# One decoder layer with attention, convolution and experts: the part between attention and the first expert is ordered anew

## The reference

```python
mod = silu(c) @ w_ada + b_ada                 # shift, scale, gain for both halves (6 x 1024)
sh1, sc1, g1, sh2, sc2, g2 = split(mod, 6)
mix = mixer(x * (1 + sc1) + sh1)              # attention A (4 heads), attention B (8 heads), conv C, then w_out
x = layer_norm(ALPHA * x + g1 * mix, ln_g[0], ln_b[0])
h = x * (1 + sc2) + sh2
logits = h @ w_router + b_router              # 32 experts, best 4, softmax over the 4
y = sum over the 4 of gate * expert(h)        # expert: 1024 -> 2048, clamped SwiGLU, 1024 -> 1024
x = layer_norm(ALPHA * x + g2 * y, ln_g[1], ln_b[1])
```

## Time and profile before

| | us |
|---|---|
| three runs | 1288.34, 1290.24, 1290.70; median 1290.24 |
| profiled execution | 1290.84 |
| its span | 1289.1 |
| PE busy | 1026.4 |
| DVE busy | 317.9 |
| ACT busy | 183.3 |
| DMA queue of SP | 449.26 MB, 86.0% of 16 engines' span |

### The profile page before, as it was taken

The page is one execution under the profiler, slowest core; times in us unless marked ns, Lnnn a source line. Parts: engine busy times, 40 slices in busy tenths (PEclk is TensorE's granted clock), DMA queues, the critical chain, the costliest instruction groups (busy, mean ns, idle before and its releaser), DMA issues.

```text
span 1289.1 us, 30824 instructions
## 1 busy us (share of the span) xinstructions
PE 1026.4 (80%) x12341; PEld 487.2 (38%) x12342; DVE 317.9 (25%) x1042; ACT 183.3 (14%) x512; POOL 55.0 (4%) x137
## 2 busy tenths in 40 slices
PE   3799897498997877868698969997896897867872
PEld 2455653343443332423343433442343343332331
DVE  0295456712211211211121211121111111111215
ACT  0101332411111100101011101110111111110101
POOL 2900000000004000000000000000000000000000
PEclk9799899599998977988899989999898999888987
DMA  9987773279999999999799899089979979999993
GB/s 325 335 293 267 222 274 157 102 294 421 420 420 420 420 420 421 420 420 396 329 421 419 338 419 418 8 339 420 413 319 419 421 326 420 421 419 421 422 420 138
DMA packets 78075, 455.05 MB, mean 353 GB/s; under 512 B 9067, under 2 KB 16661, under 8 KB 28769
## 3 DMA queue, kind: packets, MB, share of 16 engines
q1 hardware_dynamic: 73840, 449.26, 86.0%
q10 hardware_dynamic: 4145, 4.41, 1.1%
HBM read 451.59 MB, written 2.61 MB: 352 GB/s over the span
## 4 chain that ended last, share of the span: by engine, by line
PE 38%; DMA 24%; SPq 22%; DVE 8%; issue 5%; ACT 2%; ACTq 0%; DVEq 0%
DMA w<-in_w_e_out 22%; PE bank L1677 15%; SPq L407 10%; PE bank L1705 8%; SPq L410 6%; PE bank L1658 3%; SPq L388 2%; PE comb L1637 2%; PE bank L1548 1%; DMA w<-in_ln_b 1%; SPq L374 1%; DMA w<-in_w_ada 1%; PE bank L1693 1%; PE bank L1670 1%; SPq L483 1%
## 5 line engine op out<-in xcount | busy, mean ns | idle before, releaser
L1677 PE MATMUL bank<-w,mt 128*32 128x512 f32 x3264 | 389.6, 622 | 45.8 <-DMA w<-in_w_e_in 45.8
L1705 PE MATMUL bank<-w,mt 128*32 128x256 f32 x3264 | 197.2, 387 | 45.8 <-DMA w<-in_w_e_out 31.8
L1677 PEld LDWEIGHTS bank<-w,mt 128*32 128x32 f32 x3264 | 96.4, 113 | 301.2 <-issue 215.8
L1224 DVE TENSOR_SCALAR mt<-bank 128x256 f32<-128x256 f32 x51 | 21.6, 424 | 718.6 <-PE bank L1677 718.6
L1705 PEld LDWEIGHTS bank<-w,mt 128*32 128x32 f32 x3264 | 98.7, 111 | 127.6 <-DMA w<-in_w_e_out 48.1
L1658 PE MATMUL bank<-pick,hb 128*128 128x32 bf16 x2448 | 80.2, 179 | 67.3 <-issue 64.2
L1658 PEld LDWEIGHTS bank<-pick,hb 128*128 128x128 bf16 x2448 | 75.4, 97 | 91.8 <-issue 91.8
L823 ACT ACTIVATE mt<-mt 128x256 f32<-128x256 f32 x51 | 21.3, 417 | 493.5 <-DVE mt L1224 493.5
L1637 PE MATMUL comb<-mt,gpickT 32*128 32x256 f32 x832 | 80.9, 462 | 0.5 <-ACT mt L830 0.5
L1659 PE MATMUL bank<-pick,hb 96*128 96x32 bf16 x408 | 72.5, 179 | 0.0
L1637 PEld LDWEIGHTS comb<-mt,gpickT 32*128 32x128 f32 x832 | 35.4, 199 | 49.2 <-issue 46.5
(11 more groups left out here) (335 smaller groups left out, 816.2 us busy)
## 6 DMA issues: line engine op xcount, KB each, us to landing
w<-in_w_e_in SPq DMA_DIRECT2D x256, 1024.0 KB, 26.0
w<-in_w_e_out SPq DMA_DIRECT2D x128, 1024.0 KB, 21.3
w<-in_w_ada SPq DMA_DIRECT2D x12, 2048.0 KB, 11.0
w<-in_w_in SPq DMA_DIRECT2D x3, 2048.0 KB, 21.9
w<-in_w_in SPq DMA_DIRECT2D x2, 1024.0 KB, 21.5
w<-in_w_out SPq DMA_DIRECT2D x4, 512.0 KB, 10.1
w<-in_w_out SPq DMA_DIRECT2D x2, 1024.0 KB, 12.3
w<-mod_rows SPq DMA_DIRECT2D x4, 512.0 KB, 6.6
```

Of the source, the lines that this page charges most:

```text
L1677: ins = mm(quarter(bank[0][SLOTS * q:SLOTS * (q + 1), :], 0), xT[:, SLOTS * k:SLOTS * (k + 1)], quarter(slot[s], q), start=False, stop=(k ...
L1705: ins = mm(bank[0][SLOTS * q:SLOTS * (q + 1), 0:256], hid, slot[s][:, D * (k % 2) + 256 * q:D * (k % 2) + 256 * (q + 1)], start=False, sto ...
```

## The change

It does the following, in one kernel:

- the sample's values go on three column tiles of PE (24 products of 128 columns), with three ACT copies; the first projection waits for its input piece by piece, and the sample's input lies in quarters on 128 partitions;
- attention takes all of tile 0 first, then tile 1; the output projection starts after step 6 and has 28 products within attention instead of 20; the sample's projection comes ahead of the last four products of tile 1;
- DVE waits for `ld["brow"]` ahead of the first `maxima`; the first tile's layer norm sits in steps 11, 12 and 13 of attention;
- the sample's layer norm works on 128 partitions by 256 columns; the layer norm's scaling is folded into two passes for each half; the tiles are taken in the order 0, 2, 1; `choose` has 9 small operations;
- the first block is written out ahead of the loops; the visiting order is multiplied behind its first products, and `cum`, `order` and the clearing of sums come inside it; expert 0 has at least two blocks (`minblk`);
- the end: two loads on a semaphore `gain`, four on `final`; the last layer norm is done by DVE in two fused passes, with ACT doing the root only; POOL applies the mean and root to the rows kept for it.

```diff
-        h2rows = [h2row, W1[1][:, 14336:15360], W1[1][:, 15360:16384]]
+        hbq = [MT[:, 3328 + 128 * j:3456 + 128 * j].bitcast(BF16) for j in range(2)]
+        h2rows = [h2row, W1[1][:, 14336:15360], W1[1][:, 15360:15616]]
...
-        ATT = [("A", t, j) for t in range(2) for j in range(2)] + [("B", t, i) for t in range(2) for i in range(4)] \
+        ATT = [(kind, t, i) for t in range(2) for kind, n in (("A", 2), ("B", 4)) for i in range(n)] \
...
-        ORD = (0, 1, 2)
+        ORD = (0, 2, 1)
-        OP_AFTER = {7: (0, 0, 3), 8: (0, 3, 6), 9: (0, 6, 9), 10: (0, 9, 12), 11: (0, 12, 14), 12: (0, 14, 16), 13: (1, 0, 4)}
+        OP_AFTER = {6: (0, 0, 3), 7: (0, 3, 6), 8: (0, 6, 9), 9: (0, 9, 12), 10: (0, 12, 14), 11: (0, 14, 16), 12: (1, 0, 4), 13: (1, 4, 8), 14: (1, 8, 12)}
...
# SP
-                sp.dma_start(dst[0:32, 1, :], mod_dram[1:2, D * at:D * (at + 1)].to_broadcast([32, D])).then_inc(ld["brow"], 16)
+                quarters = bass.AP(tensor=mod_dram.tensor, offset=mod_dram.offset + 6 * D + D * at, ap=[[256, 4], [0, 32], [1, 256]])
+                sp.dma_start(dst[:, 1, 0:256], quarters).then_inc(ld["brow"], 16)
-            sp.wait_ge(part3, 3)
+            sp.wait_ge(part3, 5)
...
# ACT, attention and behind it
                 if s + 2 < NATT:
                     exps(s + 2)
+                if s == 12:
+                    a.activation(warm[0:1, 0:1], warm[0:1, 1:2], ACT.Sqrt)
+                if s == 13:
+                    root(0, 1)
...
             first_part(0)
-            root(1)
             second_part(0)
+            third_part(0)
+            root(2, 2)
+            copy_h2T(0)
+            sample_part(0)
+            root(1, 3)
+            stack_sample(0)
+            copy_h2T(2)
+            a.activation(warm[0:1, 0:1], warm[0:1, 1:2], ACT.Exp)
             first_part(1)
-            copy_h2T(0)
-            third_part(0)
-            root(2)
...
+            sample_part(1)
+            gate_exp(0)
+            gate_exp(2)
+            stack_sample(1)
             second_part(1)
+            stack_sample(2)
             third_part(1)
+            gate_exp(1)
...
# DVE
+            dve.wait_ge(ld["brow"], 6 * 16)
             for s in logits_in(0):
                 maxima(s)
             normalise(0)
...
                     if n < NATT:
                         maxima(n)
+                if s == 11:
+                    ln_half(0, 0)
+                elif s == 12:
+                    ln_half(0, 1)
+                elif s == 13:
+                    ln_rest(0)
             copy_o(NATT - 1)
...
+            def shifted(t, parts):
+                g = GROUP[t]
+                for rows, row, c in parts:
+                    ins = v.scalar_tensor_tensor(out=row, in0=rows, scalar=cstat[:, t, 0:1], in1=sc2b[:, g, c], op0=ALU.subtract, op1=ALU.mult)
+                link(ins)
+                inverse(t, ORD.index(t) + 1)
+                for rows, row, c in parts:
+                    v.scalar_tensor_tensor(out=row, in0=row, scalar=cstd[:, t:t + 1], in1=sh2b[:, g, c], op0=ALU.mult, op1=ALU.add).then_inc(h2_ready, 1)
...
-            dve.wait_ge(ld["brow"], 6 * 16)
             dve.wait_ge(ld["wr"], 32)
-            ln_half(0, 0)
-            ln_half(0, 1)
-            ln_rest(0)
+            residual(0, 0)
             ln_half(1, 0)
-            residual(0, 0)
+            ln_sample_sums()
+            residual(0, 1)
+            ln_sample_rest()
             ln_half(1, 1)
             ln_rest(1)
-            residual(0, 1)
+            residual(2, 0)
             choose(0)
-            ln_half(2, 0)
-            ln_half(2, 1)
-            ln_rest(2)
-            residual(1, 0)
-            choose(1)
-            residual(2, 0)
-            residual(1, 1)
             choose(2)
             residual(2, 1)
+            residual(1, 0)
+            ranks(0)
+            ranks(2)
+            residual(1, 1)
+            choose(1)
+            ranks(1).then_inc(m["pick"], 1)
...
+            gated_picks(slice(0, SLOTS), 2)
+            dve.wait_ge(order_done, 1)
+            v.tensor_copy(cum[:, 3:NE + 3], bank[3][0:1, 352:384]).then_inc(cum_ready, 1)
+            v.tensor_copy(order[:, :], bank[3][0:1, 320:352]).then_inc(cum_ready, 1)
+            activate(1, 2)
...
# PE, values of the sample
+                        for k in range(DK):
+                            for q, a in enumerate((W_VA, W_VA + P, W_VB)):
+                                ins = mm(ps[32 * q:32 * q + 32, 0:P], hT[:, k, SEQ:NTOK], win[:, k, a:a + P],
+                                         start=(k == 0), stop=(k == DK - 1))
...
# PE, behind attention
-            out_proj(1, 4, 16)
             pe.wait_ge(o_copied, NATT)
             for k in range(DK):
                 for q in range(4):
                     ins = mm(bank[3][32 * q:32 * q + 32, 0:256], hT[:, k, SEQ:NTOK], w2v[:, k, 256 * q:256 * (q + 1)],
                              start=(k == 0), stop=(k == DK - 1))
             ins.then_inc(op_done, 1)
+            out_proj(1, 12, 16)
...
+            h2_transposes(0)
+            router(0)
+            for t in (2, 1):
+                h2_transposes(t)
+                router(t)
...
+                if opening:
+                    visiting_order()
+                else:
+                    combine(1)
+                    combine(2)
...
+            block_work(0, 1, turns, 1, 2, opening=True)
+            load_ends(pe, ends)
+            pe.wait_ge(y_zero, 2)
...
# DVE, the end
-            dve.wait_ge(ld["final"], 6 * 16)
-            dve.wait_ge(quad_done, 1)
+            dve.wait_ge(ld["gain"], 2 * 16)
             total_rows(0)
+            total_rows(2)
...
             statistics(0)
...
+            dve.wait_ge(ld["final"], 4 * 16)
+            centred(0, XY[:, 0, :], lng2)
+            inverse(0, 4)
+            scaled(0, XY[:, 0, :], lnb2)
```

More of the change, by code:

```diff
@@ L215, in hybrid_streaming_encoder_step @@
             "c", "x", "cs", "ka", "kb", "v", "tabs", "cln", "sinks", "be", "wr", "ext", "toep", "wout",
-            "brow", "final")}
+            "brow", "gain", "final")}
         ld_win = [sem(f"ld_win{j}") for j in range(4)]
@@ L663, in _ @@
                     t = int(name[1])
-                    ins = a.activation(vtok[0:TS[t], t, :], ps[0:TS[t], 0:384], ACT.Copy)
+                    if t < 2:
+                        ins = a.activation(vtok[:, t, :], ps[:, 0:384], ACT.Copy)
+                    else:
+                        for q in range(3):
+                            ins = a.activation(vtok[0:32, 2, P * q:P * (q + 1)], ps[32 * q:32 * q + 32, 0:P], ACT.Copy)
                 else:
@@ L733, in _, with root @@
             exps(1)
+            def root(t, n):
+                eng.wait_ge(ln_var, n)
+                a.activation(cstd[:, t:t + 1], cstat[:, t, 1:2], ACT.Sqrt).then_inc(ln_std, 1)
             for s in range(NATT):
@@ L778, in _, with gate_exp @@
+            def gate_exp(t):
+                eng.wait_ge(top_done, ORD.index(t) + 1)
+                a.activation(gate[:, t, :], lg[:, t, :], ACT.Exp, bias=rs[:, t:t + 1]).then_inc(gexp_done, 1)
             first_part(0)
-            root(1)
             second_part(0)
+            third_part(0)
[6 more added lines that the diff above has]
+            a.activation(warm[0:1, 0:1], warm[0:1, 1:2], ACT.Exp)
@@ L837, in _ @@
             for i, t in enumerate(FIN):
-                eng.wait_ge(fin_var, i + 1)
-                a.activation(cstd[:, t:t + 1], cstat[:, t, 1:2], ACT.Sqrt).then_inc(fin_std, 1)
-                eng.wait_ge(fin_shift, i + 1)
-                rows = x1q if t == 2 else XY[:, t, :]
-                a.activation(rows, rows, ACT.Identity, bias=rs[:, t:t + 1], scale=cstd[:, t:t + 1]).then_inc(fin_norm, 1)
+                root(t, 4 + i)
         @block.vector
@@ new lines, in ranks @@
+            def ranks(t):
+                i = ORD.index(t)
+                dve.wait_ge(rank_done, max(i + 1, 2))
+                dve.wait_ge(mask_done, i + 1)
+                link(v.scalar_tensor_tensor(out=rank[:, t, :], in0=bank[4][:, 128 + NE * t:128 + NE * (t + 1)], scalar=1.0,
+                                            in1=maskb[:, t, :], op0=ALU.add, op1=ALU.mult))
+                r = TS[t] if t < 2 else 96
+                return v.tensor_scalar(pick[0:r, t, :], iota[0:r, 0:SLOTS], rank[0:r, t, 0:1], None, ALU.is_equal)
@@ L1196, in moe @@
-                v.tensor_scalar(sel[:, j, :], eye3[:, col(which)].to_broadcast([96, SLOTS]), 1.0, None, ALU.mult)\
-                 .then_inc(sel_ready, 1)
-                dve.wait_ge(m["pick"], picked)
-                v.tensor_scalar(rkc[:, :, :], rank[:, :, col(which)], 1.0, None, ALU.mult).then_inc(cur_ready, 1)
-                v.tensor_scalar(gtc[:, :, :], gate[:, :, col(which)], 1.0, None, ALU.mult).then_inc(cur_ready, 1)
+                    if not isinstance(e, int):
+                        free = dve.snap(dve.value_load(cum[0:1, col(e + 1)], min_val=0, max_val=160) + 1, min_val=1, max_val=161)
```

(5 more changed lines are left out.)

648 lines of the change are left out of this document (318 added, 330 removed).

## The result

| | kernel before | changed kernel |
|---|---|---|
| runs | 4, median 1289.84 us (1288.34 to 1290.70) | 4, median 1304.97 us (1302.38 to 1306.05) |
| profiled execution, span | 1290.84, 1289.1 us | 1304.88, 1303.1 us |
| DVE, ACT, POOL busy | 317.9, 183.3, 55.0 us | 310.6, 181.1, 65.1 us |

The ratio is 1.0117, with a 95% interval of 1.0104 to 1.0130: slower, by 15.1 us. The prediction had 1298.9 and the range 1290.5 to 1307.

A forecast was written before the change was run, and what follows sets the result against it. No engine is saturated up to the first block, which sets everything after; transfers bound the light experts. +31.3 + 2.8 - 22.7 + 1.3 - 4.0 = +8.7 gave 1298.9 us beside the median, range 1290.5 to 1307.

The forecast's parts named there:

- The landing of the rows: Start to attention's first transposes: DVE's wait for the modulation rows moves them from 150.85 to 182.2, +31.3 us.
- about 3 us earlier, last landing at 179.1: Modulation-row loads behind ACT's state stores: last landing at 179.1 in place of 182.1, bounds 182.5 and 177.
- Attention: First transposes to the end of attention, today 52.2 us: +2.8 (0 to +6).
- The term of -0.9: Attention's first steps, at granted clock 0.54: the heavy logits of tile 1 leave them, -0.9 us.
- the long pause costs more: Rival: array stays at the lower level through light first steps, ACT's queue delays transposes; +4 and +4, 1307; chance 0.18.
- From attention's end to the first products: Attention's end to the first expert products: 33.3 us in place of 56.0, -22.7.
- ACT, named as the risk: Behind attention: ACT's one queue, twelve small copies and a root waiting for tile 1; 4 us lost to 2 won.
- The first block: Inside the first block: order's products and casts +0.7, expert 0's range read in the open +0.6; +1.3 (0.5 to 3).
- The tail: The end: DVE starts at 1265.3, -3.05, then 17.3 us of passes in place of 18.3; -4.0 (-2.5 to -5).
- The early gate: Rival at SP's wait for state stores: they drain in 5 us, not 20, sum falls by 14 to 1285; chance 0.09.
- the cancelling halves: Rival: way behind attention 4 us shorter, or attention gains from its order, and rows land at 177; 1290; chance 0.10.
- the way not shortened: Rival behind attention: the router's and DVE's latencies stay, -12 in place of -22.7; 1309.6; chance 0.05.

The follow-up runs named there:

- the run with the early gate: Changed kernel with ACT's two stores of the convolution states issued ahead of its eight stores of values and keys: 1301.53 us, ratio 1.0100.
- the last version: Changed kernel with the `brow` wait in step 11, attention's old step order, and first output products waiting for six copied steps, not eight: 1267.06 us, ratio 0.9838.
- the changed kernel with the extra instructions: Changed kernel plus one register instruction at each of the loads of the ends of the first two experts: 1302.87 us, ratio 1.0115.
- the late wait: Changed kernel with DVE's wait for `brow` moved from ahead of the first maxima to step 11: 1267.93 us, ratio 0.9840; second set 1270.21 us.
- the run with the old wait: Changed kernel with the `brow` wait in step 11 and DVE's last part waiting for all six loads again: 1272.13 us.
- the kernel before with the early wait: Kernel before with only the `brow` wait moved ahead of the first maxima: 1319.38 us, ratio 1.0241.

## Why the prediction was right or wrong

**Right, and shown:** the wait for the modulation rows ahead of the first maxima turns the change from a gain into a loss. Moving it to step 11 gives 18 to 20 us below the kernel before, putting it into the kernel before costs 31.4. The measured 1304.97 lies in the range of 1290.5 to 1307, but 1 us above the band of 1294 to 1304 that had a chance of 0.58. All terms but attention's were within 3 us, and the errors, +2.7, +3.2, -1.8, +0.7, +0.7 and -0.3, add up to +5.2, which is, but for rounding, the distance from +8.7 to +14.0.

**The landing of the rows, +31.3 forecast, +34.0 measured.** The step that missed is "about 3 us earlier, last landing at 179.1"; it was 181.7, near the bound of 182.5 that was named for a total traffic unchanged, but not for that reason. Three small terms ate the gain. ACT issued its second state store 1.5 earlier, not 3.1 (145.92 for 147.47): the sample's values began 0.7 later in this profile (137.40 for 136.66), and from their start to that store ACT and PE needed 2.3 less and not 3.1. From that store the drain took 21.4 us in both kernels, so the stores' end did follow their own start. The six issues took 0.5 longer from first to last (167.38 to 170.09, against 168.91 to 171.16), and the last row landed 11.6 after its issue, against 10.9. The equal packet counts of the two queues were thus read rightly for ACT's stores; but they say nothing of rows that are issued early, for these stand in SP's queue behind SP's own weights: in the run with the early gate issues earlier by 16 us gain 3.4 at most. The Trainium skill (DMA: Bandwidth & Descriptors, Queues, rings and completion order) says that on each DMA engine the descriptors of one ring are consumed in the order of the ring; the run with the early gate agrees, where weights fill SP's queue until 170 and the last row, issued at 162.29, lands at 182.15. From landing to first transposes the forecast was 3.1 and 3.13 was measured.

**Attention, +2.8 forecast, +6.0 measured.** The term for four more output products ahead of the last values was right (3.7 forecast; one step's four take 3.63). The term of -0.9 is the one that missed: it should have been +2.3 here. It took the stretch at the lower level as given and reasoned that light steps are cheap in it. But with the new order that stretch is longer in most profiles: in eight profiles with the new order two to four steps are slow (four in five of them, three in two, two in one), in five with the old order always two. With four, the new order's seven steps ahead of the first output products take 18.7 us (184.89 to 203.62), as long as the old order's eight (18.7 in the last version). So the step that has moved behind that point costs its 2.5 us there, and the light steps do not give them back. With two slow steps they do: in the changed kernel with the extra instructions the seven steps take 15.4 us (186.01 to 201.36) and attention 54.8, where the forecast had 52.2 + 2.8 = 55.0. That the pause does it (the rival "the long pause costs more") is refuted: after 5 us and after 41 us of pause the same four steps are slow, two are slow after 41 us in the run just named, and in the kernel before attention takes 52.2 after a pause of 3.3 and 52.0 after one of 34.5. Why one execution has two and another four stays open; the Trainium skill (TensorE: Matmul & The Clock Gate, What's actually happening) says that the number of slow matmuls varies from run to run of one kernel, and the profiles agree.

**From attention's end to the first products, -22.7 forecast, -24.5 measured.** By the start of the first product in PE's timeline the stretch is 31.0 to 31.5 us in all eleven profiles of kernels with the new way, and 55.8 and 55.9 in the two with the old. The plan held to within 2 us at each point: the sample's and tile 1's products 10.9 (10.8 forecast), tile 1's transposes at 18.3 (18.5), the last choice at 27.9 (29.5), the first products at 31.5 (33.3). What was overpriced lies ahead of the last choice: tile 1's router products end at 23.8 and not 24.8, and the ranks and the residual that follow at 26.0 and not 27.6. ACT, named as the risk, costs one visible stall (2.8 us ahead of the sample's router products), which is in the shadow of tile 1's passes on DVE. No run takes the edits on this way apart, so what each of them gives is not shown.

**The first block, +1.3 forecast, +2.0 measured.** The pause between first and second products grew by 0.4 (2.9 to 3.3: the order's products and casts). The read of the range in the open does not show. In its place the first products take 9.12 us against 7.44, the array being at the lower level again after the router's short products (granted clock 0.50 from 274 to 278, where the kernel before had 0.80 from 258 to 262); in the late wait these took 7.62, but the second products 5.35 in place of 3.66. In these two profiles it is 1.7 to 1.9 us, over all eleven of the new way 1.0 to 2.4 (both groups of products together, against 11.1 in the kernel before); the forecast lacked this term.

**The tail, -4.0 forecast, -4.3 measured, for another reason in part.** The pieces were -3.1 for DVE's start and -1.1 for fewer passes, and both came. That the first fits is partly luck: the run with the old wait shows that two loads ahead of the others give 0.8 of the 3.1; the other part comes with the six loads being issued earlier: the last issue ended 5.4 us ahead of the last prompt combination in the kernel before, and 10.1 ahead of it in the run with the old wait. (In the kernel before with the early wait it was 7.2, and DVE started 1.4 behind the combination.)

**The rivals.** The early gate (0.09) is refuted by a run, the cancelling halves (0.10) did not happen, the long pause (0.18, 1307) has the nearest time but the wrong cause, and its second half, 4 us lost on ACT behind attention, did not come, the way not shortened (0.05) is refuted by the two traces. A better version than both kernels exists: the change with the wait at step 11, at 1268 to 1270 us, 18 to 20 us below the kernel before. With attention's old order it is 1267.1 to 1268.1. That the order itself gains is not shown: attention takes 55.4 to 56.9 in the three profiles of the old order with these output products, and 54.8 to 58.4 in the eight of the new one.

## What to carry to other kernels

A wait belongs ahead of the first instruction that needs the data; moved ahead of a loop it makes everything that is queued behind it on that engine, and on those that wait for it, as late as the slowest transfer, and here it turned a gain of 18 to 20 us into a loss of 15. Before a load is brought forward by opening its gate, look at what the same queue has issued ahead of it: that is the second gate. When the time moves against the intent of a large change, cut both ways, the suspect out of the new kernel and into the old one; where the parts are small, read the stretch in the trace and not the median, and in several executions: attention's stretch alone took 54.8 to 58.4 us in eight profiles with the same steps.

## What was not expected of the hardware

- In the late wait PE had an instruction in flight all the time from 155 to 160 (5.00 of 5.00 us busy) and the array was at the lower level throughout (0.50); the slow steps lasted 12 us. The same instructions left it within 5 us in the changed kernel with the extra instructions (186.01 to 191.00).
- An issue on SP's queue took 2.5 to 7.6 us in place of 0.3 to 0.6 for the same six loads when they followed 4 MB of expert weights by 11 us (the run with the early gate). SP's next load, of expert 0, came at 169.88, only 0.9 earlier than without the early gate (170.74), or 4.7 when both are counted from SP's first four pieces of expert 0, though the first row had been issued 16 us earlier by that count.
